# A GpSimd queue that feeds split weights and gathers rows: the gathers one v tile later, two or fewer a tile

## The chip, the cores and the metric

The kernel runs on one core of a Trainium2 chip. The metric is the device time of that core in microseconds (us). It is an FP32 kernel of 56826 recorded instructions, one launch for the whole reference.

## The reference, cut to what matters

One inference step of a decoder layer for 288 tokens (256 of a prompt, 8 sequences of 4): adaLN and RMSNorm, an RWKV-7 mixer beside an mLSTM mixer, an output projection, and then a PEER feed-forward, which is where the change stands. PEER has 16384 experts of 2048 numbers in two tables `u` and `v`; every token picks 128 of them:

```python
s_top, i_top = lax.top_k(s, PEER_TOPK)
...
idx = jnp.take_along_axis(cand_i, pos, axis=-1)...      # 128 experts of a token
gate = jax.nn.softmax(best_s, axis=-1)...
ue = jnp.take(u, it, axis=0)
act = jax.nn.gelu(jnp.einsum('nd,ned->ne', xt, ue), approximate=False) * gt
ve = jnp.take(v, it, axis=0)
return jnp.einsum('ne,ned->nd', act, ve)
```

The result is normed once more and is the output `y`.

## The kernel before

The kernel does not gather `u`: it multiplies all 288 tokens with all of `u` (128 tiles), and keeps the activations of all experts. For `v` it goes two ways. The first 208 tokens (`VN`) take the dense way: their activations, zero where an expert isn't picked, are multiplied with all of `v`, in 128 **v tiles** (`LATE_TILES`, numbered m = 0 to 127) of 1 MB of weights each. The last 80 tokens (`GATHERED`) take the gathered way: for each of these tokens the 128 picked rows of `v` are fetched from DRAM and multiplied with the 128 picked activations. This goes in 40 **steps** (`STEPS`), a step being half of the columns (h) of four tokens; a group j of four tokens is steps 2j and 2j + 1.

Numbers are FP32 but go through TensorE in two parts of a faster format. For each v tile n four engines work in turn:

- SyncE (SP) loads the weights into a ring of four slots, the load of tile m behind the end of tile m - 4 on TensorE.
- ScalarE (ACT) writes the high part of the weights, in two halves, and of the activations (line 1686). The first half for tile m + 2 waits until TensorE is half through tile m (`half_used`), the second until it is through with it. In the first and the last tile of a pass of eight the order of the matmuls is another one, and `half_used` comes near the tile's end.
- GpSimd (POOL) subtracts to get the low part of the first 640 columns (`lo_front`, line 813). VectorE (DVE) does the rest (line 2782) and the low part of the activations (line 2779).
- TensorE (PE) runs 32 matmuls (line 929) for the tile, once it has GpSimd's low part and VectorE's.

GpSimd has a second duty in its queue, which runs in program order. Behind `lo_front` of tile m it issues gathers by indirect DMA: for each token one of 128 **late activations** (`picked_acts`, line 898), and for each token and half one of 128 **rows** of 4 KB (`rows_in`, line 905, 512 KB each, four to a step). Two row buffers, one for each h, hold four gathers; so those of step s + 2 wait until TensorE has used step s (`rows_used`). The first late activation of a group waits for `picks_ready`: for VectorE's multiply of the group ahead by its gates (`spread_picks`, line 2805). VectorE does `spread_picks(j)` behind its subtractions of tile `gathered_after(2j)` + 1, once the four late activations of group j have landed. TensorE runs step s (16 matmuls on `rows_in`) right behind v tile `gathered_after(s)`, once the spread activations and the rows are there; these tiles are 9, 11, 14, 17, 20, 22, 25, 28, 31, 34, 36 and so on to 118, two or three apart. So what is due when on GpSimd is set by two functions alone, `acts_begun(m)` and `gathers_begun(m)`: what is issued behind `lo_front(m)`.

Of the kernel before, what the change touches and what calls it, by code (L numbers as in the profile page):

```python
# [109 lines left out]
STEPS = GATHERED // 2  # L110
# [86 lines left out]
def build(nc, T):  # L197
    ctx = ExitStack()
    with ctx:
# [277 lines left out]
        def gathered_after(step):  # L477

            return 9 + step * (LATE_TILES - 19) // (STEPS - 1)
# [4 lines left out]

        def acts_begun(m):

            first = {6: range(4)}.get(m, ())
            return [*first] + [4 * j + i for j in range(1, GATHERED // 4) for i in range(4)
                               if m == gathered_after(2 * j - 2) + 1 + i]

        def gathers_begun(m):

            if 2 <= m <= 4:
                return [(i // 4, i % 4) for i in range(3 * (m - 2), min(3 * (m - 1), 8))]
            at = [(step, m - gathered_after(step)) for step in range(STEPS - 2) if 0 < m - gathered_after(step) <= 2]
            return [(step + 2, g) for step, nth in at for g in range(2 * nth - 2, 2 * nth)]

        assert sorted(x for m in range(LATE_TILES) for x in gathers_begun(m)) == [(g, i) for g in range(STEPS) for i in range(4)]
        assert [t for m in range(LATE_TILES) for t in acts_begun(m)] == [*range(GATHERED)]
        TURNED = 6  # L500
        assert TURNED * GATHERED <= 512
# [288 lines left out]
        def _(pool):  # L790
# [97 lines left out]
            for m in range(LATE_TILES):  # L888
                lo_front(n_late + m)
                if m == 2:  # L890
                    pool.wait_ge(S("picks_copied"), 2)
                    pool.wait_ge(used, n_late)
                elif m == 6:
                    pool.wait_ge(S("side_moved"), 16 + 64)
                for t in acts_begun(m):
                    if t % 4 == 0 and t:
                        pool.wait_ge(S("picks_ready"), 1 + t // 4)
                    pool.indirect_dma_start(picked_acts[:, t:t + 1], None, late_acts,  # L898
                                            bass.IndirectOffsetOnAxis(ap=pick_at[:, 2, t:t + 1], axis=0)
                                            ).then_inc(S("side_done"), 16)  # L900
                for step, g in gathers_begun(m):
                    t, h = 4 * (step // 2) + g, step % 2
                    if step >= 2:
                        pool.wait_ge(S("rows_used"), 4 * EARLY_BODIES + step - 1)
                    pool.indirect_dma_start(rows_in[h][g], None, v_halves,  # L905
                                            bass.IndirectOffsetOnAxis(ap=pick_at[:, h, t:t + 1], axis=0)
                                            ).then_inc(S(f"rows{h}_landed"), 16)
# [2090 lines left out]
```

## Time and profile before

| | us |
|---|---|
| median of 3 runs | 2697.5 (2695.27 to 2701.05) |
| profiled execution | 2691.04 |
| its span | 2689.2 |
| first matmul of v tile 0 | 1921.5 |
| step 0 on TensorE begins | 1981.6 |
| step 39 on TensorE begins | 2621.3 |
| last matmul of v tile 127 ends | 2671.3 |

All times of rows are counted from the span's start. A row of a time line gives start, duration, engine, line, operation, what is written and read, and in square brackets how long the engine had been idle and who ended that. TensorE overlaps the end of a matmul with the next one, so the starts of tiles tell more than their busy time. [...] In rows of waits the columns are the sum, the number and the longest wait. In the groups below PEld is TensorE's weight load, which runs ahead of the matmuls; a wait of PEld is no loss as long as PE has work.

### The profile page before, as it was taken

What the parts mean: (1) busy time and instruction counts of PE and PEld (TensorE: products, weight loads), DVE (VectorE), ACT (ScalarE), POOL (GpSimd) and SP (SyncE); (2) the same over time, 40 slices, a digit from 0 to 9 for tenths busy, and PEclk for the clock granted to TensorE, in tenths of its full rate; (3) what the DMA queues carried; (4) which work ended last, traced back from release to release, by engine and by line L of the source; (5) the groups of instructions that cost most, each with busy time, mean ns of one, the idle gap of its engine ahead of it and who ended that gap; (6) DMA issues with size and microseconds to landing.
All of it is one profiled execution on the core that took longest, in us unless ns stands there. A gap on an engine that the chain in (4) does not pass through costs nothing.

```text
span 2689.2 us, 56826 instructions
## 1 busy us (share of the span) xinstructions
PE 2552.9 (95%) x23437; PEld 2349.3 (87%) x23437; DVE 1376.5 (51%) x2443; ACT 1084.5 (40%) x1752; POOL 1617.1 (60%) x844
## 2 busy tenths in 40 slices
PE   5899999989979999999999999999989999999997
PEld 3799999657757999999999999999978888888887
DVE  0550355773236456994573110010377777767777
ACT  1332433341223434544333333333444555445555
POOL 0366676123125776888546777877657767767663
PEclk9799999889988999999999999999999999999999
DMA  9987844587764444445546555654679898999884
GB/s 374 393 283 271 283 162 156 192 288 243 249 225 160 172 160 138 158 165 181 178 171 230 205 194 202 222 185 168 246 275 315 311 360 310 322 337 311 302 291 130
DMA packets 213561, 639.92 MB, mean 238 GB/s; under 512 B 16520, under 2 KB 26264, under 8 KB 183832
## 3 DMA queue, kind: packets, MB, share of 16 engines
q1 hardware_dynamic: 176712, 514.54, 55.4%
q0 software_dynamic: 27472, 97.56, 10.0%
q10 hardware_dynamic: 9216, 25.53, 2.4%
q8 instruction: 118, 1.93, 0.3%
q14 instruction: 43, 0.35, 0.0%
HBM read 605.61 MB, written 31.97 MB: 237 GB/s over the span
## 4 chain that ended last, share of the span: by engine, by line
PE 63%; POOL 17%; issue 10%; DVE 5%; DMA 4%; ACT 1%; POOLq 0%; SPq 0%; DVEq 0%; ACTq 0%
PE bank L929 62%; POOL ring_lo L806 8%; POOL staged L905 5%; POOL ring_lo L813 3%; DMA kept<-in_w_ada 3%; POOL staged L898 1%; DMA kept<-in_peer_v 1%; DVE ring_lo L2782 1%; DVE act_hl L2779 1%; PE bank L932 0%; DMA staged<-in_w_ada 0%; ACT hi_peer L1686 0%; DVE staged L2366 0%; DVE staged L2844 0%; DVE staged L2390 0%
## 5 line engine op out<-in xcount | busy, mean ns | idle before, releaser
L1686 ACT ACTIVATE hi_peer<-kept 128x1024 fp32r<-128x1024 f32 x544 | 559.3, 1054 | 927.0 <-PE bank L929 854.3
L806 POOL TENSOR_TENSOR ring_lo<-kept,hi_peer 128x1024 fp32r<-128x1024 f32 x288 | 718.6, 2517 | 271.0 <-ACT hi_peer L1686 271.0
L929 PE MATMUL bank<-h_hi,ring_lo 128*128 128x288 f32 x2848 | 840.0, 295 | 0.0
L929 PE MATMUL bank<-act_hl,hi_peer 128*128 128x416 f32 x2048 | 632.9, 373 | 25.9 <-POOL ring_lo L813 20.6
L929 PE MATMUL bank<-h_hi,hi_peer 128*128 128x288 f32 x2048 | 609.4, 298 | 2.9 <-POOL ring_lo L806 2.6
L929 PE MATMUL bank<-h_lo,hi_peer 128*128 128x288 f32 x2048 | 605.3, 296 | 0.0
L929 PEld LDWEIGHTS bank<-h_hi,ring_lo 128*128 128x128 f32 x2848 | 538.1, 189 | 0.0
L929 PE MATMUL bank<-act_hl,ring_lo 128*128 128x208 f32 x2048 | 530.5, 259 | 0.0
L929 PEld LDWEIGHTS bank<-act_hl,hi_peer 128*128 128x128 f32 x2048 | 386.8, 189 | 74.1 <-issue 36.3
L929 PE MATMUL bank<-staged 64*64 64x64 f32 (+13 forms) x6760 | 386.6, 298 | 30.0 <-issue 18.5
L2779 DVE TENSOR_TENSOR act_hl<-staged,act_hl 128x416 fp32r<-128x416 f32 x256 | 257.8, 1007 | 292.2 <-ACT act_hl L1686 291.5
L929 PEld LDWEIGHTS bank<-act_hl,ring_lo 128*128 128x128 f32 x2048 | 394.3, 193 | 0.0
L929 PEld LDWEIGHTS bank<-h_hi,hi_peer 128*128 128x128 f32 x2048 | 384.2, 188 | 4.6 <-POOL ring_lo L806 4.5
L929 PEld LDWEIGHTS bank<-h_lo,hi_peer 128*128 128x128 f32 x2048 | 384.7, 188 | 0.0
L806 POOL TENSOR_TENSOR ring_lo<-kept,hi_front 128x1024 fp32r<-128x1024 f32 x100 | 244.1, 2462 | 217.1 <-ACT hi_front L1686 217.1
L929 PEld LDWEIGHTS bank<-staged 64*64 64x64 f32 (+7 forms) x6760 | 271.6, 138 | 113.4 <-issue 76.8
L905 POOL DMA_INDIRECT staged<-in_peer_v,staged x160 | 197.8, 1236 | 107.4 <-PE bank L929 71.4
L813 POOL TENSOR_TENSOR ring_lo<-kept,hi_peer 128x640 fp32r<-128x640 f32 x128 | 206.9, 1620 | 77.5 <-ACT hi_peer L1686 75.7
L2782 DVE TENSOR_TENSOR ring_lo<-kept,hi_peer 128x384 fp32r<-128x384 f32 (+1 forms) x256 | 252.9, 988 | 0.0
L929 PE MATMUL bank<-h_hi,hi_front 128*128 128x288 f32 x800 | 241.7, 302 | 0.1
L929 PE MATMUL bank<-h_lo,hi_front 128*128 128x288 f32 x800 | 237.8, 297 | 0.0
L2772 DVE TENSOR_TENSOR staged<-staged 128x832 f32 (+1 forms) x24 | 44.2, 1842 | 317.7 <-ACT staged L1683 183.3
(261 smaller groups left out, 3106.3 us busy)
## 6 DMA issues: line engine op xcount, KB each, us to landing
kept<-in_peer_u SPq DMA_DIRECT2D x128, 1024.0 KB, 4.8
kept<-in_peer_v SPq DMA_DIRECT2D x128, 1024.0 KB, 8.0
kept<-in_w_ada SPq DMA_DIRECT2D x64, 1024.0 KB, 8.8
kept<-in_w_in SPq DMA_DIRECT2D x50, 1024.0 KB, 4.9
staged<-in_w_ada SPq DMA_DIRECT2D x32, 1024.0 KB, 6.5
kept<-in_w_adaf SPq DMA_DIRECT2D x32, 1024.0 KB, 5.9
kept<-in_w_out SPq DMA_DIRECT2D x16, 1024.0 KB, 5.0
kept<-in_w_q SPq DMA_DIRECT2D x16, 1024.0 KB, 4.8
```

What stands on the lines that cost most here:

```text
L806: pool.tensor_tensor(ring_lo[:, n % RING_SLOTS, cols], ring[n % RING_SLOTS][:, cols], hi_slot(n)[:, cols].bitcast(F32), ALU.subtract).then ...
L813: pool.tensor_tensor(ring_lo[:, n % RING_SLOTS, cols], ring[n % RING_SLOTS][:, cols], hi_slot(n)[:, cols].bitcast(F32), ALU.subtract).then ...
L898: pool.indirect_dma_start(picked_acts[:, t:t + 1], None, late_acts, bass.IndirectOffsetOnAxis(ap=pick_at[:, 2, t:t + 1], axis=0)).then_inc ...
L905: pool.indirect_dma_start(rows_in[h][g], None, v_halves, bass.IndirectOffsetOnAxis(ap=pick_at[:, h, t:t + 1], axis=0)).then_inc(S(f"rows{h ...
L929: return pe.matmul(out, lhsT, rhs, start=start, stop=stop)
L1686: return act.activation(out, in_, ACT.Copy)
L2772: tt(a, a, gates_in[slot].rearrange("p (t k) -> p k t", k=QUARTER), ALU.mult).then_inc(S("gates_applied"), 1)
L2779: tt(lo, acts_part(m, part), hi.bitcast(F32), ALU.subtract)
L2782: tt(ring_lo[:, n % RING_SLOTS, cols], ring[n % RING_SLOTS][:, cols], hi_slot(n)[:, cols].bitcast(F32), ALU.subtract).then_inc(S("acts_spl ...
```

## The change

Behind which v tile a gather is issued. Per group, late activation i moves from `gathered_after(2j - 2)` + 1 + i to + 2 + i. Per step, the four row gathers of step s + 2 stood behind the low parts of the first and the second tile after the tile of step s, two and two; now they stand behind the second (two), the third (one) and the fourth (one). The first eight row gathers go over four tiles (2 to 5) and not three; the first four late activations over tiles 6 and 7. What each instruction does, its buffers and its waits stay.

```diff
         def acts_begun(m):
 
-            first = {6: range(4)}.get(m, ())
+            first = {6: range(2), 7: range(2, 4)}.get(m, ())
             return [*first] + [4 * j + i for j in range(1, GATHERED // 4) for i in range(4)
-                               if m == gathered_after(2 * j - 2) + 1 + i]
+                               if m == gathered_after(2 * j - 2) + 2 + i]
 
         def gathers_begun(m):
 
-            if 2 <= m <= 4:
-                return [(i // 4, i % 4) for i in range(3 * (m - 2), min(3 * (m - 1), 8))]
-            at = [(step, m - gathered_after(step)) for step in range(STEPS - 2) if 0 < m - gathered_after(step) <= 2]
-            return [(step + 2, g) for step, nth in at for g in range(2 * nth - 2, 2 * nth)]
+            if 2 <= m <= 5:
+                return [(i // 4, i % 4) for i in range(2 * (m - 2), 2 * (m - 1))]
+            turns = {2: (0, 1), 3: (2,), 4: (3,)}
+            return [(step + 2, g) for step in range(STEPS - 2) for g in turns.get(m - gathered_after(step), ())]
```

Of the order of the instructions only GpSimd's changes. Its queue of the kernel before, around the first gathers behind a step; L813 is a low part and so a tile, L898 a late activation, L905 a row gather:

```order
L813 TENSOR_TENSOR ring_lo<-kept,hi_peer 128x640 x4
L898 DMA staged<-late_acts,staged 128x1
L905 DMA staged<-in_peer_v,staged 128x1024 x2
L813 TENSOR_TENSOR ring_lo<-kept,hi_peer 128x640
L898 DMA staged<-late_acts,staged 128x1
L905 DMA staged<-in_peer_v,staged 128x1024 x2
L813 TENSOR_TENSOR ring_lo<-kept,hi_peer 128x640
```

The low parts are those of tiles 7 to 10, 11 and 12. The same place in the changed kernel, with the low parts of tiles 8 to 11, 12, 13 and 14:

```order
L813 TENSOR_TENSOR ring_lo<-kept,hi_peer 128x640 x4
L898 DMA staged<-late_acts,staged 128x1
L905 DMA staged<-in_peer_v,staged 128x1024 x2
L813 TENSOR_TENSOR ring_lo<-kept,hi_peer 128x640
L898 DMA staged<-late_acts,staged 128x1
L905 DMA staged<-in_peer_v,staged 128x1024
L813 TENSOR_TENSOR ring_lo<-kept,hi_peer 128x640
L898 DMA staged<-late_acts,staged 128x1
L905 DMA staged<-in_peer_v,staged 128x1024 x3
L813 TENSOR_TENSOR ring_lo<-kept,hi_peer 128x640
```

The first gathers behind step 0 (tile 9) came behind the low part of tile 10 and now come behind that of tile 11. Where two steps are two tiles apart (9 and 11), three row gathers fall on one tile, here 13: the last of the one step and two of the next. Ahead of that, on GpSimd in v tiles 2 to 7:

```order
-L905 DMA staged<-in_peer_v,staged 128x1024 x3
-L813 TENSOR_TENSOR ring_lo<-kept,hi_peer 128x640
-L905 DMA staged<-in_peer_v,staged 128x1024 x3
-L813 TENSOR_TENSOR ring_lo<-kept,hi_peer 128x640
-L905 DMA staged<-in_peer_v,staged 128x1024 x2
-L813 TENSOR_TENSOR ring_lo<-kept,hi_peer 128x640 x2
-L898 DMA staged<-late_acts,staged 128x1 x4
+L905 DMA staged<-in_peer_v,staged 128x1024 x2
+L813 TENSOR_TENSOR ring_lo<-kept,hi_peer 128x640
+L905 DMA staged<-in_peer_v,staged 128x1024 x2
```

Ahead of the low part of tile 3 stand two row gathers and no longer three.

## Rows read from the trace of the kernel before

**Rows 1.** Busy time in the stretch from step 0 to step 39:
```profile
1981.60:2621.40 639.80, 615.73 (x4116) 538.19 (x4120) 473.40 (x583) 322.31 (x436) 450.02 (x338) 1.00 0.91 317
```

**Rows 2.** Who waited for whom in the same stretch:
```profile
POOL staged L905 <- PE bank L929: 71.4, 34, 3.3
...
POOL staged L898 <- DVE staged L2805: 56.1, 19, 5.8
ACT hi_peer L1686 <- DMA kept<-in_peer_v: 51.5, 17, 5.0
...
PEld bank L929 <- POOL ring_lo L813: 32.4, 43, 2.4
...
PE bank L929 <- POOL ring_lo L813: 18.7, 36, 2.2
...
PE bank L929 <- DVE staged L2805: 5.0, 7, 1.9
```

**Rows 3.** The chain that ended last, 2060 to 2110, by line:
```profile
by line: PE bank L929 41.0%; POOL staged L905 25.3%; POOL ring_lo L813 20.2%; POOL staged L898 7.3%; issue 7.3%
```

**Rows 4.** Time line of GpSimd, tile 24's activation, then tiles 26 to 28:
```profile
2068.09 1.36 POOL L898 DMA_INDIRECT staged<-late_acts,staged  x1 [0.16 <-issue]
...
2080.90 1.95 POOL L905 DMA_INDIRECT staged<-in_peer_v,staged  x1 [1.57 <-PE bank L929]
...
2084.12 1.57 POOL L813 TENSOR_TENSOR ring_lo<-kept,hi_peer 128x640 fp32r<-128x640 f32 x1
2085.85 1.14 POOL L898 DMA_INDIRECT staged<-late_acts,staged  x1 [0.16 <-issue]
2087.30 1.25 POOL L905 DMA_INDIRECT staged<-in_peer_v,staged  x1 [0.30 <-issue]
...
2089.82 1.57 POOL L813 TENSOR_TENSOR ring_lo<-kept,hi_peer 128x640 fp32r<-128x640 f32 x1
```

**Rows 5.** Time line of TensorE: step 6, starts of tiles 26, 27, 28; of 121, 127:
```profile
2078.68 1.92 PE L929 MATMUL bank<-staged 128*32 128x512 f32 x16
2080.53 0.46 PE L929 MATMUL bank<-act_hl,hi_peer 128*128 128x416 f32 x1
...
2085.74 0.45 PE L929 MATMUL bank<-act_hl,hi_peer 128*128 128x416 f32 x1 [0.16 <-POOL ring_lo L813]
...
2091.44 0.46 PE L929 MATMUL bank<-act_hl,hi_peer 128*128 128x416 f32 x1 [0.62 <-POOL ring_lo L813]
...
2637.43 0.37 PE L929 MATMUL bank<-act_hl,hi_peer 128*128 128x416 f32 x1
...
2666.31 0.36 PE L929 MATMUL bank<-act_hl,hi_peer 128*128 128x416 f32 x1
```

**Rows 6.** Time line of ScalarE, the high part for tile 28:
```profile
2083.22 1.06 ACT L1686 ACTIVATE hi_peer<-kept 128x1024 fp32r<-128x1024 f32 x1 [2.94 <-PE bank L929]
```

**Rows 7.** Step 24 on TensorE, and the stretch in which it ran (columns as rows 1):
```profile
2376.09 3.62 PE L929 MATMUL bank<-staged 128*32 128x512 f32 x16 [1.94 <-DVE staged L2805]
...
2376.20:2379.50 3.30, 3.30 (x16) 0.50 (x14) 1.64 (x4) 2.69 (x4) 0.97 (x1) 0.50 1.05 392
```

**Rows 8.** Landing of a late activation; of a weight tile (size, median):
```profile
DMA to landing us min/median/max: 2.4/5.9/8.1
...
kept<-in_peer_v SPq DMA_DIRECT2D x109, 1024.0 KB, 8.1
```

**Rows 9.** A stretch in which DMA also reloads activations (columns as rows 1):
```profile
2160.00:2200.00 40.00, 39.03 (x268) 33.75 (x267) 31.19 (x39) 21.16 (x29) 25.80 (x20) 1.00 1.02 369
```

**Rows 10.** v tiles 3 to 7: TensorE's, ScalarE's and VectorE's long gaps:
```profile
1938.01 0.46 PE L929 MATMUL bank<-act_hl,hi_peer 128*128 128x416 f32 x1 [1.92 <-POOL ring_lo L813]
...
1951.36 1.06 ACT L1686 ACTIVATE hi_peer<-kept 128x1024 fp32r<-128x1024 f32 x1 [4.48 <-DMA kept<-in_peer_v]
...
1964.23 0.69 PE L929 MATMUL bank<-act_hl,hi_peer 128*128 128x416 f32 x1 [4.05 <-DVE ring_lo L2782]
...
1959.67 4.42 DVE L2782 TENSOR_TENSOR ring_lo<-kept,hi_peer 128x1024 fp32r<-128x1024 f32 x1
```

## The prediction

> **What bounds the kernel now.** I read the table of stretches first. TensorE has work nearly throughout, so the place is a stretch where it should run back to back and doesn't. In the 639.8 us from step 0 to step 39 TensorE has the full clock (1.00) [rows 1]. What would this stretch take without waits? With no gathers left, six v tiles in a row start 28.88 us apart in all, 4.81 each (2637.43 to 2666.31) [rows 5]. A step costs its 1.92 and 0.1 of refill (the first matmul behind it takes 0.46 and not 0.37) [rows 5], 2.02. So 109 tiles and 39 steps make 524.3 + 78.8 = 603.1 us. The stretch loses 36.6 us.
>
> Second, the waits: TensorE's matmuls were idle 18.7 us behind GpSimd's low part in 36 waits, and 5.0 us behind VectorE's spread activations in 7 [rows 2]. Each wait costs more than its idle time: the overlap of neighbouring tiles (0.16) is lost and the refill of 0.1 comes on top. Tile by tile, 39 of the 109 tiles begin 0.05 us behind the end of their low part, as tile 27 does (low part 2084.12 + 1.57, start 2085.74) [rows 4, 5], and their start comes 28.0 us later in all than 4.81 or 6.83 behind the one ahead; 18.7 + 39 x 0.25 = 28.5 says the same. Of the rest 6.6 us stand where a step waited for its spread activations.
>
> Third, the chain that ended last: from 2060 to 2110 only 41% of it is TensorE; 25% is row gathers, 20% low parts, 7% late activations [rows 3]. It shows why GpSimd is late though only 450 of 640 us busy [rows 1]: it waits itself, 71.4 us in 34 waits for TensorE ahead of row gathers [rows 2]. The pattern is in the time line: at 2080.90, when step 6 had just ended, it issues the first gather, then a second, and only at 2084.12 comes to the low part of tile 27, done 0.05 us before TensorE starts on it; a late activation and two row gathers further, 5.70 us from low part to low part against 4.81 for a tile, it is later still, and tile 28 waits 0.62 [rows 4, 5].
>
> **The change, the wait for a step.** The low part of tile g + 2 now stands ahead of the gathers that need step g. Take a tile g with a step, starting on TensorE at 0. ScalarE begins the high part of g + 2 at 2.7 (2083.22 for tile 28, with tile 26 started at 2080.53) [rows 5, 6], 3.8 with it done; low part to 5.4; the late activation to 6.8; step g ends at 6.8, so its buffers are free as GpSimd arrives. Two row gathers of 1.25 to 1.95 and 0.3 between [rows 4] end at 10.3. The low part of g + 3 can't begin before the half of g + 1, 6.85 + 2.7 + 1.1 = 10.6, and ends at 12.3. TensorE starts g + 3 at 16.6. GpSimd is 4.3 us early where it was 0.05. Where a pass ends the half comes 1.9 later and 2.4 are left. The tiles with three row gathers and a late activation take 5.70 + 1.55 = 7.25, against 4.81 for the tile and 2.02 for its step; the surplus eats the lead of 2.4 to 4.3, not more. GpSimd's work for two steps is 5.6 low parts, 4 late activations and 8 row gathers, at 1.7, 1.4 and 1.5 some 27 us of the 31 that the floor gives: it keeps up. Of the 28.0 us I take back 26; bounds: 28, and 20 if the fuller tiles catch it.
>
> **VectorE's share of it.** With GpSimd in front, its low part begins with VectorE's first subtraction, and they hold each other up: 4.42 us for a subtraction with two low parts beside it [rows 10]. Tiles 121 to 127 ran so and kept 4.81 [rows 5]. VectorE is busy for 473 of 640 us, such holds included [rows 1], so it has room. I cost it at nothing, bounds 0 and 4 (0.3 in each of some 14 passes, whose ends need all of VectorE's work at the tile's start).
>
> **The late activations.** They are issued one tile later and must land before their step. Where groups are six tiles apart nothing changes. In 8 of 19 groups they are five apart and the last one now goes out in the step's own tile. The time line of before has the last of group 3 at 2068.09, step 6 at 2078.68 [rows 4, 5], 10.6 us for a landing of 5.9, at most 8.1 [rows 8]. One tile is 4.8 or 6.8: were the issue to move by all of it, 2.1 to 0.1 us would be missing. But GpSimd no longer stands there behind step and spread, and low part g + 5 can be done at 5.4 of tile g + 3; that leaves 11.1 us to the step, and 9.2 where g + 3 is the end of a pass (two groups). I charge 1, bounds 0 and 9. The 6.6 of waits for spread activations stay: they come from late loads, not from GpSimd's queue. One of them, 1.94 long, was followed by a clock of 0.50, and the step took 3.62 in place of 1.92 [rows 7].
>
> **DMA.** The rate rises because the time shrinks: 317 GB/s at share 0.91 [rows 1] becomes 317 x 640/608 = 334 at 0.96. Weight tiles land 8.1 after issue [rows 8]. The issue is three tiles and a step ahead of use, 16.5 us; the two high halves (1.06 each [rows 6]), those of the activations and VectorE behind them take some 5, so a load may take 11. Twice, for 8 tiles, activations are reloaded too: there the share is already 1.02 at 369 GB/s [rows 9], and 392 is the most that stands in such a row [rows 7]. Going 5% faster there, over 2 x 45 us, isn't to be had: 4 us, bounds 0 and 8. [...]
>
> **The first tiles.** Two row gathers and not three ahead of the low part of tile 3 take away its 1.92 idle [rows 10], and the lower clock that followed it. But tile 6 waits for a weight load (ScalarE idle 4.48 to 1951.36) [rows 10], whose DMA work only shifts. Tile 7 stood 4.05 behind the blocked subtraction of 4.42, when GpSimd came out of four late activations with two low parts at once [rows 10], and ran at the low clock too (first matmul 0.69, not 0.46). With two late activations a tile this goes. Each low clock at the 1.7 of [rows 7], that is 1.9 + 1.7 + 4.05 + 1.7 = 9.4 at most; of it I leave 3.4 to the loads. I take 6, bounds 2 and 10.
>
> **Sum.** -26 + 1 + 4 - 6 = -27 us. On the profiled execution 2691.04 gives 2664. The median of the runs shown stands 6.5 above it, so 2697.5 - 27 = 2670.5. All bounds at their good end give -38, at their bad end -20 + 4 + 9 + 8 - 2 = -1; they hardly fall together.
>
> **The rivals.**
> *DMA takes the gain.* If the higher rate makes every load land 3 us later, tiles and spread activations wait for ScalarE instead: ScalarE's waits for weights (51.5 us in 17 waits [rows 2]) get a chain behind them. Half of the gain goes: -13, 2684. For it: share 1.02 [rows 9]. Against: it is so in 90 of 640 us only. Chance 0.12.
> *The change doesn't do what it says.* GpSimd's wait for steps is only moved into the fuller tiles, as late. Then -5 to 0, 2695. Against it is the walk above, with 2.4 us to spare. Chance 0.05.
> *Late activations come too late, slower.* The place is `spread_picks` on VectorE: behind it in its queue stand the subtractions of the next tile, and TensorE waits for the step. If GpSimd issues the last of a group 9 us later than in my walk, all 8 close groups wait about 5 us, each with 1.7 of low clock: 54, less the gain of 27, +27, 2724. It decides against the change from 3.5 us per close group on. Chance 0.04.
> *More than forecast.* The waits for spread activations go too, as GpSimd no longer blocks VectorE at odd times: -34, 2663. Chance 0.14, inside the range.
>
> **How the numbers follow.** My forecast with its own bounds (2664 to 2680) has 0.65, the better case 0.14, the rival of DMA 0.12, the two bad ones 0.09. The range 2661 to 2687 takes in the first three but for their far ends and leaves out under 2 in 10. Within 0.2% (5.4 us) is what a measurement of this kernel can't tell from no change: faster 0.92, same 0.04, slower 0.04.
>
> **What would show it.** In the profile after, the row of TensorE's idle time behind GpSimd's line 813 between steps 0 and 39 falls from 18.7 to under 3, the wait of line 905 for PE from 71.4 to under 25, that of line 898 for VectorE from 56.1 to under 20; the stretch takes 612 to 622 us; its DMA share is 0.94 or more. ScalarE's wait for weights stays or grows. TensorE's wait for line 2805 stays under 10. I am wrong if tiles still start 0.05 us behind their low part in dozens, if steps wait for late activations in the close groups, or if ScalarE's waits for loads double.

## The result, and the profile of the changed kernel

| | before | changed |
|---|---|---|
| median of 4 runs each | 2696.88 us (2695.27 to 2701.05) | 2678.64 us (2670.88 to 2685.20) |
| ratio | | 0.9922, 95% interval 0.9905 to 0.9939 |
| profiled execution, its span | 2691.04, 2689.2 | 2670.88, 2669.1 |
| first matmul of v tile 0 | 1921.5 | 1923.1 |
| from step 0 to step 39 on TensorE | 639.7 | 618.2 |
| last matmul of v tile 127 ends | 2671.3 | 2651.1 |
| behind it to the end of the span | 18.0 | 18.0 |

The change makes the kernel 18.2 us faster by the medians and 20.1 by the spans of the profiled executions. The forecast was 27 us and 2670.5; 2678.64 lies in its range.

The stretch from step 0 to step 39 in the changed kernel. The columns are those of [rows 1]: the stretch and its length, the busy time and number of instructions of PE, PEld, DVE, ACT and POOL, the share of TensorE's full clock that was granted, the mean busy share of the DMA engines, and what they moved in GB/s.

```profile
1982.96:2601.19 618.23, 606.10 (x4113) 537.58 (x4113) 467.15 (x583) 319.90 (x435) 460.43 (x337) 1.00 0.93 328
```

Beside [rows 1] TensorE does the same work in 618.2 us and not 639.8, busy for 606.1 of them (615.7 before). GpSimd is as busy as before, 460 and 450 us. What went is its being late. The waits of the same stretch:

```profile
ACT hi_peer L1686 <- PE bank L929: 170.2, 111, 5.7
...
ACT hi_peer L1686 <- DMA kept<-in_peer_v: 116.5, 41, 5.1
POOL ring_lo L813 <- ACT hi_peer L1686: 100.0, 46, 5.1
...
DVE staged L2803 <- DMA staged<-late_acts,staged: 5.9, 2, 4.9
PE bank L929 <- DVE staged L2805: 5.6, 6, 2.7
PE bank L929 <- DVE staged L2844: 4.6, 5, 1.3
POOL staged L905 <- PE bank L929: 3.1, 5, 1.0
PE bank L929 <- POOL ring_lo L813: 1.8, 1, 1.8
...
POOL staged L898 <- DVE staged L2805: 0.9, 3, 0.4
```

Beside [rows 2], GpSimd's wait for steps fell from 71.4 to 3.1 us, that for the spread activations from 56.1 to 0.9, and its idle time now stands ahead of the low part, where it waits 100.0 us for ScalarE: it has become early. TensorE's idle time behind it fell from 18.7 us in 36 waits to 1.8 in one.

Tile by tile, much as the prediction counts them (what a tile's start comes later than 4.82, or with a step 6.84, behind the one ahead), the loss over tiles 10 to 118 fell from 35.7 to 15.6 us:

| us lost on TensorE | before | changed |
|---|---|---|
| tiles that start right behind GpSimd's low part | 28.0 (39 tiles) | 2.1 (2 tiles) |
| steps that wait for spread activations | 6.6 | 7.2 |
| tiles where a pass begins, and the rest | 1.1 | 6.3 |
| tiles 0 to 9, ahead of these | 11.7 | 10.1 |

Three places need their rows. **Step 6 is the largest single loss between steps 0 and 39.** GpSimd, VectorE and TensorE around it in the changed kernel (time lines, columns as [rows 4]):

```profile
2055.85 5.01 POOL L905 DMA_INDIRECT staged<-in_peer_v,staged  x1 [0.30 <-issue]
2060.87 1.58 POOL L813 TENSOR_TENSOR ring_lo<-kept,hi_peer 128x640 fp32r<-128x640 f32 x1
...
2066.86 0.93 POOL L905 DMA_INDIRECT staged<-in_peer_v,staged  x1 [0.30 <-issue]
2067.81 1.55 POOL L813 TENSOR_TENSOR ring_lo<-kept,hi_peer 128x640 fp32r<-128x640 f32 x1
2069.52 1.15 POOL L898 DMA_INDIRECT staged<-late_acts,staged  x1 [0.16 <-issue]
```
```profile
2055.75 1.68 DVE L2772 TENSOR_TENSOR staged<-staged 128x832 f32<-128x832 f32 x1
2057.32 0.62 DVE L2779 TENSOR_TENSOR act_hl<-staged,act_hl 128x416 fp32r<-128x416 f32 x1
2057.82 0.58 DVE L2782 TENSOR_TENSOR ring_lo<-kept,hi_peer 128x384 fp32r<-128x384 f32 x1
2058.29 0.62 DVE L2779 TENSOR_TENSOR act_hl<-staged,act_hl 128x416 fp32r<-128x416 f32 x1
2058.79 1.25 DVE L2782 TENSOR_TENSOR ring_lo<-kept,hi_peer 128x1024 fp32r<-128x1024 f32 x1
2059.93 2.81 DVE L2844 SCALAR_TENSOR_TENSOR staged<-bank,kept,staged 128x208 f32<-128x208 f32 x6
...
2076.83 0.06 DVE L2803 MEMSET staged<- 128x4 f32 x1 [4.91 <-DMA staged<-late_acts,staged]
```
```profile
2069.41 0.46 PE L929 MATMUL bank<-act_hl,hi_peer 128*128 128x416 f32 x1 [1.81 <-POOL ring_lo L813]
...
2077.15 1.92 PE L929 MATMUL bank<-staged 128*32 128x512 f32 x16 [2.67 <-DVE staged L2805]
```

The issue of one row gather takes 5.01 us, where the shortest take 0.93. It begins 0.1 after VectorE has begun a chain of TENSOR_TENSOR without a gap, and ends 0.93 behind the start of the first instruction of another kind at 2059.93, as if it had done nothing until that chain was over. Behind it comes the full tile, an activation and three rows, and low part to low part is 6.94 us. Low part 25 is done at 2069.36 and tile 25 starts 0.05 behind it, 1.81 late. The last late activation of the group stands behind that low part, goes out at 2069.52 and lands 7.3 us later, and step 6 waits 2.67.

**Step 0 waits 1.4 us** (of the 7.2 in the table), and 1.4 to 2.1 in all but one of the kernels below that move both late activations and rows. VectorE in the kernel before, then VectorE, GpSimd and TensorE in the changed one:

```profile
1981.36 0.15 DVE L2805 TENSOR_TENSOR staged<-staged 128x4 f32<-128x4 f32 x1
```
```profile
1981.36 1.50 DVE L2805 TENSOR_TENSOR staged<-staged 128x4 f32<-128x4 f32 x1
```
```profile
1980.31 2.53 POOL L813 TENSOR_TENSOR ring_lo<-kept,hi_peer 128x640 fp32r<-128x640 f32 x1 [1.42 <-ACT hi_peer L1686]
```
```profile
1982.96 1.50 PE L929 MATMUL bank<-staged 128*32 128x512 f32 x12 [1.41 <-issue]
```

The multiply that spreads the activations is a hundredth of a subtraction's size, and beside a low part of GpSimd it takes 1.50 us in place of 0.15. Before, GpSimd was still waiting at that time.

**Where a pass begins**, tiles 48, 56, 64, 72 and 112 start 0.6 to 1.5 us late, all behind VectorE. Before, three of these were 0.4 to 0.9 late, behind GpSimd's low part. VectorE, GpSimd and TensorE at tile 56, in the changed kernel:

```profile
2242.28 2.53 DVE L2779 TENSOR_TENSOR act_hl<-staged,act_hl 128x416 fp32r<-128x416 f32 x1 [0.34 <-ACT act_hl L1686]
2244.74 1.21 DVE L2782 TENSOR_TENSOR ring_lo<-kept,hi_peer 128x1024 fp32r<-128x1024 f32 x1
2245.87 3.71 DVE L2844 SCALAR_TENSOR_TENSOR staged<-bank,kept,staged 128x208 f32<-128x208 f32 x8
```
```profile
2242.78 1.57 POOL L813 TENSOR_TENSOR ring_lo<-kept,hi_peer 128x640 fp32r<-128x640 f32 x1
```
```profile
2246.91 0.42 PE L929 MATMUL bank<-act_hl,hi_peer 128*128 128x416 f32 x1 [1.34 <-DVE staged L2844]
```

VectorE has to take the finished pass's banks (L2844) before TensorE may write them anew. That stands behind both halves of VectorE's subtractions, and one of these takes 2.53 us and not 0.58, because GpSimd's low part runs beside it: over tiles 10 to 117 of this trace this subtraction (L2779) takes at most 0.65 us where no low part runs, and up to 2.54 beside one.

### The profile page after: what moved, and what is told of

Same layout as the page of the kernel before. It is cut to its first block, busy times and chain, and to the rows that moved or that the text cites. A ratio compares the mean times of both kernels' runs of the same rounds, so it can differ in the third digit from the quotient of the medians.

```text
span 2669.1 us, 56826 instructions
## 1 busy us (share of the span) xinstructions
PE 2543.1 (95%) x23437; PEld 2347.2 (88%) x23437; DVE 1368.0 (51%) x2443; ACT 1083.5 (41%) x1752; POOL 1634.2 (61%) x844
## 2 busy tenths in 40 slices
DMA packets 213561, 639.92 MB, mean 240 GB/s; under 512 B 16520, under 2 KB 26264, under 8 KB 183832
## 3 DMA queue, kind: packets, MB, share of 16 engines
q8 instruction: 118, 1.93, 0.3%
## 4 chain that ended last, share of the span: by engine, by line
PE 69%; POOL 9%; issue 9%; DMA 7%; DVE 5%; ACT 1%; POOLq 0%; SPq 0%; DVEq 0%; ACTq 0%
PE bank L929 68%; POOL ring_lo L806 8%; DMA kept<-in_peer_v 3%; DMA kept<-in_w_ada 3%; DVE ring_lo L2782 2%; DVE act_hl L2779 1%; DVE staged L2844 1%; ACT hi_peer L1686 0%; PE bank L932 0%; POOL staged L905 0%; DMA staged<-in_w_ada 0%; DVE staged L2366 0%; DMA staged<-late_acts,staged 0%; POOL ring_lo L813 0%; DVE staged L2390 0%
## 5 line engine op out<-in xcount | busy, mean ns | idle before, releaser
L929 PE MATMUL bank<-act_hl,hi_peer 128*128 128x416 f32 x2048 | 625.6, 370 | 13.9 <-DVE staged L2844 6.4
L2779 DVE TENSOR_TENSOR act_hl<-staged,act_hl 128x416 fp32r<-128x416 f32 x256 | 244.3, 954 | 275.1 <-ACT act_hl L1686 261.1
L813 POOL TENSOR_TENSOR ring_lo<-kept,hi_peer 128x640 fp32r<-128x640 f32 x128 | 213.9, 1671 | 154.6 <-ACT hi_peer L1686 152.1
L2782 DVE TENSOR_TENSOR ring_lo<-kept,hi_peer 128x384 fp32r<-128x384 f32 (+1 forms) x256 | 262.4, 1025 | 0.0
L905 POOL DMA_INDIRECT staged<-in_peer_v,staged x160 | 208.0, 1300 | 45.2 <-issue 40.5
```

The costliest lines, as they stand in the source:

```text
L813: pool.tensor_tensor(ring_lo[:, n % RING_SLOTS, cols], ring[n % RING_SLOTS][:, cols], hi_slot(n)[:, cols].bitcast(F32), ALU.subtract).then ...
L905: pool.indirect_dma_start(rows_in[h][g], None, v_halves, bass.IndirectOffsetOnAxis(ap=pick_at[:, h, t:t + 1], axis=0)).then_inc(S(f"rows{h ...
L929: return pe.matmul(out, lhsT, rhs, start=start, stop=stop)
L2779: tt(lo, acts_part(m, part), hi.bitcast(F32), ALU.subtract)
L2782: tt(ring_lo[:, n % RING_SLOTS, cols], ring[n % RING_SLOTS][:, cols], hi_slot(n)[:, cols].bitcast(F32), ALU.subtract).then_inc(S("acts_spl ...
```

## The experiments

All ratios are to the kernel before, timed beside it on the same chip, with the 95% interval. "Lost" is the tile count above, tiles 0 to 9 and 10 to 118, from one profiled execution. The diffs are against the changed kernel.

### The changed kernel once more

No edit. 

> The changed kernel as it is, once more, to see how far its executions spread. Its four executions of before this read 2670.88, 2677.06, 2680.21 and 2685.2 us, with granted clocks of 0.977, 0.972, 0.970 and 0.972, while those of the kernel before stay within 2695.3 to 2701.1. Theory: what differs from run to run is how many times an idle time of TensorE of 1 to 3 us is followed by the low clock; a mean clock lower by 0.005 is 0.01 of 2675 us at half speed, 27 us, and costs 13 us. Then time and mean clock go together over the executions. Rival: the spread comes from waits for weight loads, with the clock no guide. Expected median 2675 to 2680, some 20 us under the kernel before.

Measured: 0.9910 (0.9889 to 0.9930), median 2673.53 us of 6 runs from 2664.56 to 2683.59; lost 7.4 and 17.0. All ten runs of the changed kernel have a median of 2675.1, 21 to 22 us under the kernel before. They spread over 20.6 us, where 11 runs of the kernel before took 2692.01 to 2700.83. Over these six runs a lower mean clock goes with a longer time, loosely (0.969 at 2683.59, 0.975 at 2664.56, but 0.976 at 2672.36). What sets the spread is open. Part of it arises ahead of the change: in this profile tile 0 begins at 1928.8, in the first one at 1923.1, with the same instructions. Between the steps too, lines of a few us differ between executions of one kernel: tiles where a pass begins lose 4.4 us here and 5.8 in the first profile, and VectorE's banks (L2844) cost 3.0 us of waits and not 4.6.

### Only the row gathers moved

```diff
-                               if m == gathered_after(2 * j - 2) + 2 + i]
+                               if m == gathered_after(2 * j - 2) + 1 + i]
```

with `first` as before too. 

> Only the row gathers move (one tile later, and the first eight over four tiles); late activations stay where they stood before. Theory: the 28.0 us of tiles that began 0.05 us behind their low part came from row gathers that wait for a step ahead of a low part; so this half of the change has all of the gain, TensorE's idle time behind line 813 is under 3 us, and the one step that waited for a late activation (step 6, 2.7 us in the profile of the changed kernel) doesn't wait. Expected: as the changed kernel or 2 to 4 us faster, 18 to 25 us under the kernel before. Rival: the late activations, issued ahead of the rows of the same tile and waiting for VectorE, hold GpSimd as much (56.1 us in the profile of before); then at least half of the gain is gone, and this stands 0 to 12 us under the kernel before.

Measured: 0.9921 (0.9908 to 0.9934), median 2674.17; lost 10.2 and 15.8. Waits from 1983 to 2600 in this kernel:

```profile
POOL staged L898 <- DVE staged L2805: 59.7, 19, 4.7
...
PE bank L929 <- DVE staged L2805: 6.8, 9, 3.1
...
PE bank L929 <- POOL ring_lo L813: 1.7, 1, 1.7
...
POOL staged L905 <- PE bank L929: 1.3, 2, 0.8
```

The rows alone carry the whole gain, and steps 6 and 26 wait 0.0 and 0.2 us. GpSimd still waits 59.7 us ahead of late activations, as much as before, and it costs nothing that the runs show: with the rows gone from that tile, the low part behind the wait has room.

### Only the late activations moved

```diff
-            turns = {2: (0, 1), 3: (2,), 4: (3,)}
-            return [(step + 2, g) for step in range(STEPS - 2) for g in turns.get(m - gathered_after(step), ())]
+            at = [(step, m - gathered_after(step)) for step in range(STEPS - 2) if 0 < m - gathered_after(step) <= 2]
+            return [(step + 2, g) for step, nth in at for g in range(2 * nth - 2, 2 * nth)]
```

with the first eight rows as before too. 

> Only the late activations move (one tile later, the first four over tiles 6 and 7); row gathers stay as in the kernel before. Theory (rows carry the gain): the tile behind a step still has its row gathers between two low parts, so TensorE is still idle 12 to 19 us behind line 813; expected 0 to 5 us under the kernel before, of which the first tiles are most. Rival (late activations carry half or more): 10 to 20 us under it.

Measured: 1.0121 (1.0103 to 1.0138), median 2727.72, 31 us slower; lost 8.3 and 67.4. My expectation was wrong in sign. Its waits from 1983 to 2650, and step 6:

```profile
POOL staged L905 <- PE bank L929: 152.3, 34, 6.7
...
PE bank L929 <- POOL ring_lo L813: 32.1, 46, 3.1
...
DVE staged L2803 <- DMA staged<-late_acts,staged: 19.3, 7, 4.6
...
PE bank L929 <- DVE staged L2805: 15.0, 9, 2.9
```
```profile
2081.90 0.97 POOL L898 DMA_INDIRECT staged<-late_acts,staged  x1 [0.16 <-issue]
...
2090.59 1.16 POOL L905 DMA_INDIRECT staged<-in_peer_v,staged  x1 [6.13 <-PE bank L929]
```
```profile
2088.36 1.92 PE L929 MATMUL bank<-staged 128*32 128x512 f32 x16 [1.51 <-DVE staged L2805]
```

Two things come together. GpSimd no longer waits in pieces (for the spread, then for the step), but 152.3 us for steps alone, up to 6.7 at a time, and the low part behind is later still: 49 tiles start within 0.1 us of it, 40 before. And in the close groups (steps before tiles 26, 37, 54, 65, 82, 93, 110) the last activation now comes too late: each of these steps waits 1.5 to 2.9 us. This is the slower rival's mechanism, but that the time stands at its 2724 us is luck: the rival had 54 us from the steps and took off the gain of 27, while here the seven steps lose 17.7 us, and tiles right behind their low part 42.8 where it was 28.0 before. In the changed kernel only step 6 waits for a landing.

### The first gathers as before

```diff
-            if 2 <= m <= 5:
-                return [(i // 4, i % 4) for i in range(2 * (m - 2), 2 * (m - 1))]
+            if 2 <= m <= 4:
+                return [(i // 4, i % 4) for i in range(3 * (m - 2), min(3 * (m - 1), 8))]
```

and `first` as before. 

> The changed kernel with its first gathers as they were: three, three and two row gathers in tiles 2 to 4, and four late activations in tile 6. In the two profiles tiles 0 to 9 lose 11.7 us before and 10.1 us after, so the gentler start brought 1.6 and not the 6 that the prediction took. Theory: the first tiles are held by weight loads that share the DMA engines with eight row gathers however these are dealt out, so this is 0 to 3 us slower than the changed kernel. Rival: the new start does matter and was hidden by one bad wait (1.8 us and a low clock at tile 8 in the profiled run): 5 to 8 us slower than the changed kernel.

Measured: 0.9929 (0.9915 to 0.9944), median 2677.85; lost 11.0 and 18.2. The new start is worth 3 us by the medians of the ten runs, within what the intervals leave; the kernel before lost 11.7 there, six kernels with the new start as it is 7.3 to 10.1.

### VectorE takes one bank between its halves

```diff
-            def take_pass(p):
+            def take_pass(p, dts=range(4)):
-                for dt in range(4):
+                for dt in dts:
...
                     split_acts(m, side)
+                    if side == 0 and m and m % PASS == 0:
+                        take_pass(m // PASS - 1, range(1))
...
-                    take_pass(m // PASS - 1)
+                    take_pass(m // PASS - 1, range(1, 4))
```

> The changed kernel, with one thing else: where a pass of eight tiles begins (tiles 8, 16, ... 120), VectorE takes the first of the four banks of the pass ahead between its two halves of subtractions for that tile, not behind both. In the profile of the changed kernel tiles 48, 56, 64, 72 and 112 begin 0.6 to 1.5 us late, 5.5 us in all, each just behind VectorE's take (line 2844), and tile 8 as well (1.84). Theory: these are a new wait in the place of GpSimd's; VectorE's subtraction there had been held up by GpSimd's low part, which now runs at that moment. With the take ahead, TensorE's idle time behind line 2844 (4.6 us in 5 waits) goes to under 1 and the kernel is 3 to 6 us faster than the changed kernel, 24 to 28 us under the kernel before. Rival: the take was only the last of several things, and VectorE's second half is as late as it; then 0 to 2 us.

Measured: 0.9900 (0.9885 to 0.9915), median 2670.25; lost 8.1 and 13.7. TensorE has no wait for L2844 left between the steps (4.6 us in the changed kernel), so that wait is VectorE's order. Tiles where a pass begins still lose 2.6 us. Of the gain of 5 us over the changed kernel's ten runs the intervals leave open whether it is real: they overlap.

### The first eight rows one a tile

```diff
-            if 2 <= m <= 5:
-                return [(i // 4, i % 4) for i in range(2 * (m - 2), 2 * (m - 1))]
+            if 2 <= m <= 9:
+                return [((m - 2) // 4, (m - 2) % 4)]
```

> The changed kernel with its first eight row gathers one a tile, in tiles 2 to 9, in place of two a tile in tiles 2 to 5. Theory: tiles 0 to 9 lose 7.4 to 10.1 us since eight gathers of 512 KB share the DMA engines with the weight loads, whose first ones then take 12 to 15 us; the number of gathers per us sets it, not how they stand against the low parts. Dealt out over twice the time the loads land in 8 to 10 us, ScalarE's waits for weights before step 0 (14.9 us) halve, and the kernel gains 4 to 7 us on the changed kernel. Rival: the loads are slow in these tiles for another reason, the start of a table read in pieces of 2 KB, or the loss stands in VectorE's gate work; then 0 to 2 us.

Measured: 0.9894 (0.9876 to 0.9911), median 2670.92; lost 4.6 and 12.5. Waits from 1923 to 1983 in the changed kernel, and in this one:

```profile
ACT hi_peer L1686 <- DMA kept<-in_peer_v: 14.9, 5, 6.3
...
PE bank L929 <- DVE ring_lo L2782: 3.5, 3, 1.9
PE bank L929 <- POOL ring_lo L813: 2.1, 1, 2.1
```
```profile
ACT hi_peer L1686 <- DMA kept<-in_peer_v: 9.2, 4, 4.8
PE bank L929 <- DVE staged L2844: 2.1, 1, 2.1
PE bank L929 <- DVE ring_lo L2782: 1.4, 3, 0.6
```

ScalarE's waits for weights fall from 14.9 to 9.2 us. The four kernels with one row gather a tile (this one and three below) lose 3.6 to 6.3 us in tiles 0 to 9, the six with two a tile 7.3 to 10.1, so about half goes. It fits that 4 MB of rows asked for in four tiles hold up the weight loads beside them; the runs don't tell this apart from GpSimd's shorter work in each tile.

### The last late activation a tile earlier

```diff
-                               if m == gathered_after(2 * j - 2) + 2 + i]
+                               if m == gathered_after(2 * j - 2) + 2 + min(i, 2)]
```

> The changed kernel with the last late activation of each group one tile earlier, beside the third one, so no late activation is issued in the tile of its own step. Theory: steps 6 and 26 (the two close groups whose third tile ends or begins a pass) waited 2.7 and 0.9 us in the first profile, 2.4 and 2.4 in the second, for just this one; these waits go, 2 to 5 us. The other waits for spread activations, half a us each at tiles 49, 65 and 105, stay. Rival: the landing isn't the cause of these waits but VectorE, late by loads; then nothing changes, within 1 us.

Measured: 0.9910 (0.9896 to 0.9924), median 2673.87; lost 8.1 and 22.2. At the two steps that the edit was made for the waits went or shrank, to 0.0 at step 6 and 0.7 at step 26. But others came in their place (6.8 us for L2805 in all), and the fuller tile pays: tile 25 starts 3.11 us late behind GpSimd. Nothing is gained.

### The last three together

> The changed kernel with the three edits of the runs beside it together: the first bank taken between the halves, the first eight gathers one a tile, and the last late activation of a group one tile earlier. If the three losses are separate, the gains add up to 9 to 18 us on the changed kernel, and this stands 29 to 38 us under the kernel before, at 2659 to 2668. If each only hides the next one (weight loads, whose waits on ScalarE had grown from 51.5 to 116.5 us), then no more than 6 us.

Measured: 0.9920 (0.9906 to 0.9933), median 2673.71; lost 3.7 and 16.9. The gains don't add up.

### More DMA

A copy of 256 KB from DRAM to DRAM goes out with the load of each of tiles 12 to 117; nobody reads what it writes. Its lines stand 4 further down. The diff shows the copy alone: two more lines declare `spare` and wait for the copies at the end.

```diff
+                if 12 <= m < 118:
+                    sp.dma_start(spare[m], src[0]).then_inc(S("spare_moved"), 16)
```

> The changed kernel, which with every load of v tiles 12 to 117 also copies 256 KB from DRAM to DRAM that nobody reads: 106 transfers, 27.8 MB read and as much written, against the 203 MB that the stretch of steps 0 to 39 moves. It prices DMA: the stretch of the changed kernel ran at share 0.92 to 0.95 with ScalarE waiting 94 to 117 us for weights, against 51.5 before, but TensorE hardly waiting for it. Theory: the weight loads have only 2 to 4 us left to their limit, so with 14% more to move the share goes to 1 and the tiles follow the loads: 15 to 50 us slower than the changed kernel, and TensorE's idle time stands behind VectorE and GpSimd that wait for ScalarE. Rival: DMA still has room, and the losses left in the changed kernel (13 to 17 us between steps 0 and 39) have nothing to do with it: 0 to 6 us slower.

Measured: 0.9980 (0.9969 to 0.9991), median 2693.23: most of the gain is gone; lost 8.2 and 36.0. Its stretch 1983 to 2600 (columns as [rows 1]) and its waits there:

```profile
1983.00:2600.00 617.00, 588.11 (x3960) 519.99 (x3962) 458.84 (x569) 307.06 (x421) 455.90 (x329) 0.99 0.99 362
```
```profile
ACT hi_peer L1690 <- DMA kept<-in_peer_v: 179.0, 60, 6.4
...
PE bank L933 <- DVE staged L2809: 10.0, 12, 2.0
PE bank L933 <- DVE ring_lo L2786: 7.9, 9, 2.0
PE bank L933 <- DVE staged L2848: 7.7, 5, 3.4
```

28 MB more (667.72 and 639.92 MB in all) cost 17 us (0.9980 less the 0.9910 and 0.9922 of the changed kernel, 0.0064 of 2697). The chain is seen at its three ends: ScalarE waits longer for weights, and TensorE waits behind VectorE's subtractions (L2786 here, L2782 elsewhere), its taking of a pass (L2848) and the spread (L2809). Waits for GpSimd's low part stay at 1.9 us. Nor does SyncE send the loads late because it issues the copies too: over tiles 16 to 111 a load goes out 0.03 us (median; at most 0.83) behind the end of the tile that frees its slot, in the changed kernel 0.03 (0.08). So late loads reach TensorE by way of ScalarE and VectorE, and DMA is what the changed kernel runs into next.

### Two rows a tile behind each step

```diff
-            turns = {2: (0, 1), 3: (2,), 4: (3,)}
+            turns = {2: (0, 1), 3: (2, 3)}
```

> The changed kernel with the four row gathers of a step behind the second and the third tile after its step, two and two, in place of two, one and one: the old grouping, one tile later, so no tile has three row gathers. In four profiles tile 25 began 0.2 to 3.1 us late, or step 6 behind it 2.4 to 3.8 us, always at the place where tile 24 carries a late activation and three row gathers just ahead of the low part of tile 25, with the end of a pass beside it. Theory: the full tile is the last thing that still makes GpSimd late there; with two and two, tile 25 and step 6 lose less than 1 us together, and the kernel gains 2 to 5 us on the changed kernel. Rival: where the wait stands is set by loads and the end of the pass, and two tiles with two gathers each behind a step make as much trouble as one with three: within 1 us.

Measured: 0.9935 (0.9919 to 0.9950), median 2680.30; lost 7.3 and 23.8. Waits of TensorE from 1983 to 2610 in this kernel:

```profile
PE bank L929 <- DVE staged L2805: 12.5, 10, 3.4
PE bank L929 <- DVE staged L2844: 3.5, 2, 1.8
PE bank L929 <- POOL ring_lo L813: 1.3, 1, 1.3
```

GpSimd is no later than in the changed kernel, but the steps wait 12.5 us for their activations and not 5.6 (8.3 in the changed kernel's second profile). My expectation was a gain, and there is none. The medians are 5 us apart in favour of two, one and one, but the intervals overlap, and the pair below is only 1 us apart: that it is the better spread isn't shown.

### Pairs

VectorE's bank and the eight rows together: 

> The changed kernel with the two edits that each gained: the first bank taken between VectorE's halves where a pass begins, and the first eight row gathers one a tile. Alone they stood at ratios 0.9900 and 0.9894 to the kernel before, the changed kernel at 0.991; with the third edit (last late activation earlier), which alone brought nothing and lost 22 us in its profile between the steps, they came to 0.992. Theory: the third edit spoiled the sum, since it puts two late activations beside a full tile of GpSimd; without it the two add up: 0.987 to 0.989, 2661 to 2668 us. Rival: one hides the other, 0.990.

Measured: 0.9898 (0.9878 to 0.9919), median 2670.19; lost 6.3 and 14.7. With two and two on top: 

> The version beside it (first bank between the halves, first gathers one a tile) and the row gathers two and two, none of three. If the full tile at tile 24 costs 2 to 5 us, this is as much faster than the version beside it, 0.986 to 0.988; if not, the same as that one within 1.5 us.

Measured: 0.9901 (0.9885 to 0.9916), median 2671.43; lost 3.6 and 25.1 in its profiled execution, with 13.2 us of waits for L2805. Both are where each single edit was; the sum that I expected of the first, 0.987 to 0.989, didn't come. The best versions, eight rows one a tile or VectorE's bank first, stand at 0.989 to 0.990, some 4 us under the changed kernel, a difference that the intervals don't settle.

## Why the prediction was right, and where it was off

**The main term held.** GpSimd's low part was to take back 26 of 28.0 us; it took back 25.9. Its signs came as forecast: L813's idle time 1.8 (under 3), L905's wait 3.1 (under 25), L898's 0.9 (under 20), and the stretch took 618.2 (612 to 622). Two tiles of 109 and not 40 start within 0.1 us of their low part; the median lead is 4.05, forecast 4.3 (the prediction's own floor puts tile g + 3 at 16.45 and not 16.6, which makes it 4.1). Of the two, tile 25 is the case named as a bound, a full tile, but it took the stretched gather to get there.

**The credit was shared wrongly in words.** The walk put the rows and the late activations together. Only the rows bring the gain: 0.9921 with them alone, 1.0121 with the activations alone. The sign "L898's wait under 20" was met and says nothing of the gain, since the kernel in which it stays at 59.7 is as fast.

**Late activations, +1 (0 to 9).** Steps lost 7.2 and not 6.6: +0.6. That the 6.6 would stay was right in size, not in cause. Before, 4.3 us of waits stood at steps 4, 20 and 24, and 1.7 of low clock behind the last of them; of these 0.5 at step 20 is left. New are 2.67 at step 6, which comes from GpSimd's queue (the activation issued at 2069.52), 1.41 at step 0 and 0.90 at step 26, where VectorE is held up.

The walk for the close groups has an error that shows here. It leaves 11.1 us from the last activation to its step, and 9.2 where a pass ends. That is so only where a step stands behind tile g + 3, in three of the eight close groups. In the other five it stands behind g + 2, and by the prediction's own floor 2.0 us less are left: 9.0, and 7.1 where a pass ends, which is at steps 6 and 26. The trace has, from issue to step, 8.9 to 9.8 us in the three, 7.2 to 9.1 at steps 2, 16 and 36, and 7.6 and 7.2 at steps 6 and 26 with their waits in them, against the 7.3 that step 6's landing took. The slower rival's mechanism is real, but in most close groups only with the rows where they were.

**VectorE's share, 0 (0 to 4): the step that failed.** The prediction took tiles 121 to 127 as proof that GpSimd beside VectorE costs nothing. There no pass ends. Where one ends, VectorE's 3.71 us of taking banks stand behind the held-up subtraction. The line of pass beginnings and the rest rose from 1.1 to 6.3, +5.2, over the bound of 4. With step 0's 1.4 and step 26's 0.9 (there a subtraction took 2.32 us and not 0.55, at 2390.15), which the table counts as steps', the share is 7.5. The missed step is that a low part of GpSimd that comes in time runs beside the very instructions of VectorE that a pass and a step begin with. The bracket in the prediction, 0.3 in each of 14 passes, had the place right; it was 0.6 to 1.5 in five.

**DMA, +4 (0 to 8).** The DMA share was to be 0.94 or more; it is 0.93 at 328 GB/s. No term of its own is left for it: the sum closes without one. But the 5.2 just named may partly be its work: in the kernel with extra copies the waits for L2848 are 7.7 us in place of 4.6 (3.0 in the second profile). How to divide them between VectorE's order and late loads isn't settled: taking one bank first removes the wait for L2844, without touching the loads. ScalarE's waits for weights did double, 51.5 to 116.5 us (93.7 in the second profile), which the prediction had named as a sign of being wrong. It isn't one: ScalarE's waits for TensorE fell from 265.5 to 170.2 at the same time. It now comes sooner and waits longer for the same load.

**The first tiles, -6 (2 to 10).** They gave -1.6 in the profiled execution, and by the other kernels with the new start 1.5 to 4.4. The 1.92 ahead of tile 3 went, but tile 4 waited 1.93 behind a weight load for which ScalarE had waited 6.26; low part 6 took 4.80 us beside VectorE's subtractions, and tile 6 waited 2.13 for it; tile 7's 4.05 became 1.07, with 1.84 at tile 8 behind VectorE's banks. What did fall is the time at a granted clock of 0.50, from 10.2 us in these tiles (3.4 from 1939.2, 6.8 from 1963.1) to 3.4 (from 1970.2). Of 9.4 the prediction had left 3.4 to the loads. That was too little: about half of the loss goes only when the rows are spread further, and the runs don't show how the rest divides between loads, GpSimd and VectorE.

**The sum** of what was measured: -25.9 + 0.6 + 5.2 - 1.6 = -21.7, and with 1.6 us more ahead of tile 0, which the change doesn't touch, -20.1. That is the difference of the spans. (Over the profiles of this work tile 0 began between 1921.5 and 1935.3.) The forecast of -27 was too good by VectorE's 5.2 and the first tiles' 4.4, less the 4 charged for DMA, which were not spent: that it came this near is partly luck. The medians moved by 18.2 in the first comparison and by about 21.6 over all runs.

## What to carry to other kernels

A wait in an in-order queue costs by what stands behind it, so look for waits ahead of work that someone needs at once, and put that work first: row gathers put one tile later, behind it, gave 0.8%, while 59.7 us of waiting with nothing urgent behind it cost nothing that showed. Move things one at a time, for of two moves one may carry the gain and the other, alone, cost more than that. When a late engine becomes early, ask what it will now run beside: here a low part that GpSimd did in time held up the one engine that the start of a pass needs.

## What the runs showed of the hardware

- **The issue of an indirect gather took up to 5.05 us beside a chain of VectorE.** 5.01 us at 2055.85 in place of 0.93, until VectorE's chain of TENSOR_TENSOR was over. Seven of the fourteen traces have such issues, of 4.88 to 5.05 us; each runs beside a gapless chain and ends 0.8 us behind it. The longest in the kernel before took 3.94. Not each such chain does it: in the changed kernel VectorE's runs without a gap from 2179.22 to 2188.12, and the row gather issued at 2183.17 takes 1.30. That VectorE is what holds the long ones up is read from where they end; what tells the two cases apart is open.
- **VectorE's subtractions and GpSimd's low parts are longer beside each other.** In the changed kernel a subtraction beside a low part takes 2.53 us and not 0.58 (the kernel before: 4.42 [rows 10]), and low part 6 took 4.80 and not 1.57.
- **DMA moved 362 GB/s over 617 us.** That was in the kernel with the extra copies, at a share of 0.99; its copies, which both read and write DRAM, are counted once in it (27.8 MB more in all, where DRAM reads and writes rose by 27.8 MB each). Shorter stretches moved more. Where activations are reloaded the kernel before has 369 over 40 us [rows 9] and 384 a little earlier (2150 to 2190), both at a share of 1.02. The changed kernel has 384 over 2150 to 2190, at 1.03, with TensorE busy for 39.95 of the 40 us: the loss that the prediction expected there isn't seen. Over 10 us it moved 400 (1940 to 1950) at 1.04. What the most is, no run shows.
- **A matmul on the split parts is shorter.** At 128x288 the kernel before takes 0.30 us each for 2048 matmuls on the parts (`h_hi`, `hi_peer`) and 0.48 for the 110 on unsplit numbers (`staged`, `kept`).
- **The low clock doesn't follow each idle.** In the prediction's row 1.94 us of idle were followed by 0.50; behind the 2.67 of step 6 its 16 matmuls took 1.92, the full clock. In the changed kernel's second profile the same step waited 2.39, and 3.4 us at 0.50 followed (from 2080.7). What tells them apart is open.
